# Hybrid trunk kernel: the start of the mixers block, the state copy on ScalarE, the last layer norm, and turnings of the identity between the first tile's products

## The reference, cut to what matters

```python
proj = h @ w_in                                   # c_q, k_a, v_a, k_i, w_i, q_b, z_f, i_b, g_b
c_q = rms_norm(c_q, cq_gain)
q_a = (c_q @ w_uq).reshape(B, L, A_HEADS, A_HEAD_DIM)
# (A) indexer: score = sum_h relu(q_i . k_i) * w_i, top 256 keys per query, softmax with ALiBi over them
# (B) HGRN2, chunkwise:
logf = logaddexp(log(lb), log1p(-lb) + log_sigmoid(z_f));  k_b = (1 - lb) * sigmoid(-z_f)
inter = einsum('bhtd,bhde->bhte', qn * exp(b), S)          # S starts at zero
intra = einsum('bhts,bhse->bhte', scores, vn)
S = exp(b_last) * S + einsum('bhsd,bhse->bhde', kn * exp(b_last - b), vn)
o_b = rms_norm(o_b, onorm_gain) * silu(g_b)
mix = concatenate([o_a, o_b]) @ w_out
h = layer_norm(ALPHA * h + mix, ...);  h = layer_norm(ALPHA * h + swiglu(h), ...)
# layer 1: a causal pooling mixer, then again layer_norm, swiglu, layer_norm; the 16 meta rows are dropped
```

## Time and profile before

| | us |
|---|---|
| median of 3 runs | 2665.35 (2661.79 to 2667.26) |
| the profiled execution's own time | 2666.79 |
| its span, first to last instruction | 2665.0 |
| PE busy, with matmuls | 2548.1 (96%) |
| DVE busy | 1290.3 (48%) |
| ACT busy | 844.5 (32%) |
| POOL busy | 1063.0 (40%) |
| mean granted TensorE clock | 0.967 of 2.4 GHz |

### The profile page before, as it was taken

One profiled execution on the slowest core, in us unless ns is written; L12 is line 12 of the kernel. 1 busy time (PEld: TensorE's weight loads), 2 busy tenths in 40 slices (PEclk: granted clock), 3 DMA queues, 4 the chain that ended last, 5 costly groups with the idle time before them and its releaser, 6 DMA issues.

```text
span 2665.0 us, 36229 instructions
## 1 busy us (share of the span) xinstructions
PE 2548.1 (96%) x14090; PEld 2180.5 (82%) x14090; DVE 1290.3 (48%) x2460; ACT 844.5 (32%) x1387; POOL 1063.0 (40%) x624
## 2 busy tenths in 40 slices
PE   7899999789999989999999999999999999999996
PEld 6789999667788778899888777888787888888885
DVE  6789999588886423333333323332232332232224
ACT  3675221333333223222222322322332322332221
POOL 0432213364544414344434433444433444455442
PEclk9899999699999999999999989999998999999998
DMA  4101220333233234333323223233322233333331
GB/s 133 32 17 43 89 92 19 99 92 116 87 107 96 88 103 119 96 95 95 87 72 95 80 63 95 65 110 95 95 79 79 79 101 103 94 91 103 113 103 46
DMA packets 274613, 230.87 MB, mean 87 GB/s; under 512 B 10640, under 2 KB 255440, under 8 KB 274448
## 3 DMA queue, kind: packets, MB, share of 16 engines
q1 hardware_dynamic: 266256, 220.07, 27.7%
q10 hardware_dynamic: 8192, 8.52, 0.9%
HBM read 215.81 MB, written 12.71 MB: 86 GB/s over the span
## 4 chain that ended last, share of the span: by engine, by line
PE 59%; DMA 1%; POOL 1%; DVE 1%; ACT 1%; issue 0%; POOLq 0%; SPq 0%; ACTq 0%; DVEq 0%
PE banks L1959 36%; PE banks L1975 20%; PE banks L1992 1%; PE banks L1997 1%; PE banks L2009 1%; DMA cq_raw<-in_w_up 0%; PE banks L1668 0%; DMA last_draw<-in_w_down 0%; POOL dL L1877 0%; POOL wL L1866 0%; POOL wL L1870 0%; PE banks L1994 0%; DVE y L1641 0%; DVE y L2165 0%; ACT dH L2059 0%
## 5 line engine op out<-in xcount | busy, mean ns | idle before, releaser
L1870 POOL TENSOR_TENSOR wL<-cq_raw,wH 128x2048 fp32r<-128x2048 f32 x87 | 405.7, 4664 | 565.7 <-ACT wH L2053 565.7
L1959 PE MATMUL banks<-hL,wH 128*128 128x512 f32 (+1 forms) x1760 | 618.9, 352 | 5.6 <-ACT hid L2068 5.3
L1959 PE MATMUL banks<-hH,wL 128*128 128x512 f32 (+1 forms) x1760 | 618.0, 351 | 0.0
L1959 PE MATMUL banks<-hH,wH 128*128 128x512 f32 (+1 forms) x1760 | 616.1, 350 | 0.0
L2145 DVE TENSOR_TENSOR hid<-hid,banks 128x512 f32<-128x512 f32 (+1 forms) x110 | 64.3, 585 | 742.8 <-PE banks L1959 639.2
L1959 PEld LDWEIGHTS banks<-hL,wH 128*128 128x128 f32 x1760 | 331.3, 188 | 54.9 <-ACT hid L2068 6.5
L1959 PEld LDWEIGHTS banks<-hH,wL 128*128 128x128 f32 x1760 | 331.2, 188 | 46.4
L1959 PEld LDWEIGHTS banks<-hH,wH 128*128 128x128 f32 x1760 | 331.8, 189 | 44.9
L1877 POOL TENSOR_TENSOR dL<-last_draw,dH 128x1024 fp32r<-128x1024 f32 x88 | 220.8, 2509 | 350.6 <-ACT dH L2059 350.6
L2165 DVE TENSOR_TENSOR y<-y,banks 128x512 f32<-128x512 f32 (+1 forms) x340 | 233.1, 686 | 219.9 <-PE banks L1975 218.8
L1975 PE MATMUL banks<-dH,hidL 128*128 128x512 f32 (+1 forms) x748 | 303.9, 406 | 2.3 <-issue 2.3
(11 more groups left out here) (249 smaller groups left out, 4248.0 us busy)
## 6 DMA issues: line engine op xcount, KB each, us to landing
cq_raw<-in_w_gate SPq DMA_DIRECT2D x88, 512.0 KB, 4.6
cq_raw<-in_w_up SPq DMA_DIRECT2D x88, 512.0 KB, 6.0
last_draw<-in_w_down SPq DMA_DIRECT2D x88, 512.0 KB, 3.4
w_out_part<-in_w_out SPq DMA_DIRECT2D x60, 512.0 KB, 4.0
va<-in_w_in SPq DMA_DIRECT2D x10, 1024.0 KB, 5.5
va<-in_x SPq DMA_DIRECT2D x8, 512.0 KB, 4.4
vg_scratch<-y ACTq DMA_DIRECT2D x32, 128.0 KB, 1.7
y<-in_x SPq DMA_DIRECT2D x8, 512.0 KB, 7.5
```

What stands on the lines that cost most here:

```text
L1870: nc.gpsimd.tensor_tensor(wL[:, ff % 2, :, :, :].rearrange("p g k f -> p (g k f)"), raw[:, :, :, :].rearrange("p g k f -> p (g k f)"), wH[ ...
L1959: last = nc.tensor.matmul(banks[:, GU + (2 * q + g) % 3, 0:n], wt[:, ff % 2, g, k, :], h[:, k, a:a + n], start=(k == 0 and part == 0), sto ...
```

## The change

It has five parts.

1. `w_uq` is loaded in `projection`, into a part of `y` that is free there (`w_qa0`), and scaled there by ScalarE behind the bank copy of the eighth last unit. In `mixers`, tile 0's `qa` reads it there, and a transfer copies it to `w_qa` for the other tiles. The loads of `y` wait for that copy.
2. The start of `mixers`: the fills of `zt` and `qt` go; `gates` of tile 0 work on the 64 columns that carry data (`own`); VectorE fills half of `key`, `qaT`, and after the gates `S`; GpSimd fills `vt`, `gt`, `qp`.
3. `out` of tile 0 leaves out the product with the old state, which is zero.
4. In every tile ScalarE copies the shared job of step 3 (`state`) ahead of the exponentials.
5. The last norm: ScalarE copies the gain into two PSUM banks in phase 3, VectorE multiplies from there, and for the last tile adds the bias itself, in two halves, each with a store of its own.

And TensorE turns the identity into a bank that nobody reads: once ahead of tile 0's `qa`, 14 times behind it, and 7 times behind each of tile 0's first four steps. `qa` now comes ahead of `gram` level 0.

```diff
@@ projection
+            if j == len(SLABS) - 2:
+                sp.dma_start(w_qa0, ins["w_uq"][0].rearrange("(k p) f -> p k f", p=P)).then_inc(w_qa_loaded, 16)
...
+                if m == len(slab_units) - 8:
+                    act.wait_ge(w_qa_loaded, 16)
+                    for h in range(A_HEADS):
+                        at = w_qa0[:, :, h * HD:(h + 1) * HD]
+                        nc.scalar.activation(at, at, ACT.Copy, scale=HD ** -0.5 / SLOPES[h]).then_inc(w_qa_scaled, 1)
@@ mixers, SyncE
-        sp.dma_start(w_qa[:, :, :], ins["w_uq"][0].rearrange("(k p) f -> p k f", p=P)).then_inc(w_loaded, 16)
-        sp.wait_ge(pads, 1)
         load_z(0)
-        sp.wait_ge(pads, 2)
         load_q(0)
-        sp.wait_ge(pads, 5)
+        sp.dma_start(w_qa[:, :, :], w_qa0).then_inc(w_loaded, 16)
+        sp.wait_ge(pads, 3)
...
+        sp.wait_ge(w_loaded, 16)
+        sp.wait_ge(shared_psum, nth["qa", 0])
         for m in range(5):
             load_y(m)
@@ mixers, GpSimd
-        nc.gpsimd.memset(zt[:, :], PAD_Z).then_inc(pads, 1)
-        nc.gpsimd.memset(qt[:, :], 0.0).then_inc(pads, 1)
-        nc.gpsimd.memset(qp[:], 0.0).then_inc(pads, 1)
         nc.gpsimd.memset(vt[:, 0, :], 0.0).then_inc(pads, 1)
         nc.gpsimd.memset(gt[:, :], 0.0).then_inc(pads, 1)
-        pool.wait_ge(pads, 5)
+        nc.gpsimd.memset(qp[:], 0.0).then_inc(pads, 1)
+        pool.wait_ge(pads, 3)
@@ mixers, TensorE
+                        if m:
+                            nc.tensor.matmul(banks[:, SHARED, h * HD:(h + 1) * HD], qp[:, s, par, f * P:(f + 1) * P],
+                                             state[:, f, par * HD:(par + 1) * HD], start=True, stop=False)
                         last = nc.tensor.matmul(banks[:, SHARED, h * HD:(h + 1) * HD], S[:, s, h, :],
-                                                vt[:, s, h * HD:(h + 1) * HD], start=False, stop=True)
+                                                vt[:, s, h * HD:(h + 1) * HD], start=(m == 0), stop=True)
...
+        def idle(n):
+
+            for _ in range(n):
+                nc.tensor.transpose(banks[:, T_HI, 0:P], ident[:, :], ident[:, :])
+
+        idle(1)
+        on_shared("qa", 0)
+        idle(14)
         gram(0, 0)
-        on_shared("qa", 0)
         for i, (m, h) in enumerate(steps):
             if i < NU:
                 qk(i)
                 if i and h <= levels_of(m):
                     gram(m, h)
+                if m == 0 and h < levels_of(m):
+                    idle(7)
@@ mixers, ScalarE
-        gates(0, 2)
-        gates(0, 3)
-        act.wait_ge(w_loaded, 16)
-        for h in range(4):
-            scaled(h)
-        gates(0, 4)
-        gates(0, 5)
-        for h in range(4, A_HEADS):
-            scaled(h)
+        for stage in (2, 3, 4, 5):
+            gates(0, stage)
         off_shared("qa", 0)
...
-            early = shared_job(m, h) if h == 5 else None
+            early = shared_job(m, h) if h in (3, 5) else None
@@ trunk, the last norm
+            if ph.nth == 3 and i == HALF + 2:
+                act.wait_ge(n3.gb_loaded, 32)
+                for half in range(2):
+                    at = slice(half * 512, (half + 1) * 512)
+                    nc.scalar.activation(gain_bank[:, at], n3.gb[:, at], ACT.Copy).then_inc(gain_kept, 1)
...
+    def gains_from(self, dve, j, gain, halves=False):
+
+        m = self.tiles[j]
+        dve.wait_ge(self.scaled, j - self.before + 1)
+        if not halves:
+            self.nc.vector.tensor_tensor(self.y[:, m, :], self.y[:, m, :], gain, ALU.mult).then_inc(self.gained, 1)
+            return
+        for half in range(2):
+            at = slice(half * 512, (half + 1) * 512)
+            self.nc.vector.tensor_tensor(self.y[:, m, at], self.y[:, m, at], gain[:, at], ALU.mult).then_inc(self.gained_half, 1)
+            dve.wait_ge(self.gained_half, half + 1)
+            self.nc.vector.tensor_tensor(self.y[:, m, at], self.y[:, m, at], self.bb[:, at], ALU.add).then_inc(self.biased_half, 1)
```

More of the change, by code:

```diff
@@ L60 @@
 LEVELS = 7
+SLOPES = [2.0 ** (-8.0 * (h + 1) / A_HEADS) for h in range(A_HEADS)]
 ROUNDS_AHEAD = {NT - 2: 8, NT - 1: 0}
@@ L133, in build, with projection @@
             trunk(nc, c, sem, sb, banks, ident, ins, y, hH, hL, raw, draw, out)
-def projection(nc, c, sem, sb, banks, ident, x, meta, w_in_v, ins, score, cqT, kaT, va, y, qz_dram, vg_dram, kiT, masks):
+def projection(nc, c, sem, sb, banks, ident, x, meta, w_in_v, ins, score, cqT, kaT, va, y, qz_dram, vg_dram, kiT, masks, w_qa0):
     NX = 3
@@ L675, in _, with mixers @@
                 nc.vector.match_replace(at, top8[:, m, :], at, TAKEN).then_inc(late_taken, 1)
-def mixers(nc, c, sem, sb, banks, ident, x, meta, ins, score, masks, cqT, kaT, va, y, qz_dram, vg_dram, raw, draw):
+def mixers(nc, c, sem, sb, banks, ident, x, meta, ins, score, masks, w_qa0, cqT, kaT, va, y, qz_dram, vg_dram, raw, draw):
     W = 4 * P
@@ L707, in mixers @@
     dist = sb(c, "dist", [P, L])
-    SLOPES = [2.0 ** (-8.0 * (h + 1) / A_HEADS) for h in range(A_HEADS)]
     zt = sb(c, "zt", [P, W])
@@ L1092, in on_shared @@
             if what == "qa":
-                if m == 0:
-                    pe.wait_ge(w_scaled, A_HEADS)
+                if m == 1:
+                    pe.wait_ge(w_loaded, 16)
+                w = w_qa if m else w_qa0
                 for ft in range(4):
                     for k in range(QC):
-                        last = nc.tensor.matmul(banks[:, SHARED, ft * P:ft * P + n], w_qa[:, k, ft * P:(ft + 1) * P],
+                        last = nc.tensor.matmul(banks[:, SHARED, ft * P:ft * P + n], w[:, k, ft * P:(ft + 1) * P],
                                                 cqT[:, k, t0:t0 + n], start=(k == 0), stop=(k == QC - 1))
@@ L1752, in trunk @@
                                                    sem("mixed"), sem("tail_kept"))
-    stored = sem("stored")
+    stored, gain_kept = sem("stored"), sem("gain_kept")
+    gain_bank = banks[:, PB:PB + 2, :].rearrange("p b f -> p (b f)")
     HALF = 4
@@ L1855, in _ @@
                 store(i - 4)
-        for j in range(HALF, 2 * HALF):
+        for j in range(HALF, 2 * HALF - 1):
             store(j)
-        sp.wait_ge(stored, 16 * 2 * HALF)
+        t0 = TILES[NT - 1][0] - N_META
+        for half in range(2):
+            at = slice(half * 512, (half + 1) * 512)
+            sp.wait_ge(n3.biased_half, half + 1)
+            sp.dma_start(out[0, t0:t0 + P, at], y[:, NT - 1, at]).then_inc(stored, 16)
+        sp.wait_ge(stored, 16 * (2 * HALF + 1))
     @block.gpsimd
@@ L2235, in _, with last_adds @@
                     n2.low(dve, T - 8)
-        for T in range(HALF + 2):
-            if T < HALF:
-                for half in range(2):
-                    add(NPAIR - 1, 2 * T + half)
-                dve.wait_ge(y_added, PH[-1].down(PAIRS - 1, 2 * T + 1) + 1)
-                n3.stats(dve, HALF + T)
-            if 1 <= T <= HALF:
-                n3.factors(dve, HALF + T - 1)
-            if T >= 2:
-                n3.gains(dve, HALF + T - 2)
+        def last_adds(T):
+            for half in range(2):
+                add(NPAIR - 1, 2 * T + half)
+            dve.wait_ge(y_added, PH[-1].down(PAIRS - 1, 2 * T + 1) + 1)
+            n3.stats(dve, HALF + T)
+        last_adds(0)
+        last_adds(1)
+        n3.factors(dve, HALF)
+        last_adds(2)
+        n3.factors(dve, HALF + 1)
+        dve.wait_ge(gain_kept, 2)
+        n3.gains_from(dve, HALF, gain_bank)
+        last_adds(3)
+        n3.factors(dve, HALF + 2)
+        n3.gains_from(dve, HALF + 1, gain_bank)
+        n3.factors(dve, HALF + 3)
+        n3.gains_from(dve, HALF + 2, gain_bank)
+        n3.gains_from(dve, HALF + 3, gain_bank, halves=True)
 def kernel(**inputs):
```

57 lines of the change are left out of this document (31 added, 26 removed).

## The result

| kernel | median, us | runs | ratio to before | 95% interval |
|---|---|---|---|---|
| before | 2665.99 | 2661.79 to 2667.26 | | |
| changed | 2640.12 | 2637.32 to 2645.20 | 0.9910 | 0.9893 to 0.9927 |

The change takes 25.9 us off. The profiled execution of the changed kernel took 2645.20 us (span 2643.5, clock 0.971), 5.1 above the median: its trace shows less of the gain than the runs do.

What follows compares the result with a forecast made beforehand. Outside full TensorE stretches, three places bound it: the start of `mixers`, step 3's waits for the `state` copy, and the tail. 5.0 + 9.0 + 2.5 = 16.5 us off 2666.79; 2649.5 chosen between 2650.3 and 2648.9; range 2643.5 to 2658.

Steps and rivals of the forecast that it cites:

- Start: Start of `mixers`: earlier `gram` of tile 1 and shorter `out` of tile 0 save 5.0 us at VectorE; bounds 2.3 to 7.5.
- The copy of `state`: Step 3 of each tile: copying ahead of the exponentials removes TensorE's waits, worth 9.0 us; bounds below 3 to 12.1.
- The clock behind these waits: TensorE's low clock after waits for the `state` copy: 1.5 us, counted only in the upper bound of 12.1.
- Tail: Last layer norm after TensorE's last product: gain read from PSUM and halved last tile save 2.5 us; bounds 1.5 to 4.3.
- The sum: Whole kernel: 5.0 + 9.0 + 2.5 = 16.5 us off the profiled 2666.79; forecast 2649.5, chance 0.52.
- The range: Whole kernel: from 2643.5, 1.5 below B, to 2658, halfway between A alone and A with C.
- rival B: Tile 0 and tail: clock rises and stays up into tile 1, 2.5 more; tail not held up, 1.8 more; 2645, chance 0.13.
- A: Step 3: the early `state` copy gives little, as TensorE then waits for VectorE's maxima; 3 us, about 2655.5, chance 0.19.
- C: Start of `mixers`: gives nothing, as q's transfers and GpSimd's chain set the same time; 5.0 less, 2654.5, chance 0.12.
- D: Each tile's step 3: ScalarE's early copy waits for the product, delaying exponentials; slower, about 2669.5, chance 0.04.
- E: Start: turnings don't count for TensorE's clock, so it stays low; start worth 5.0 us; within the forecast's 0.52 chance.

Runs made afterwards that it cites:

- e1: The changed kernel run again with no edit: 2642.10 us, ratio 0.9911 to the kernel before.
- e11: The changed kernel run a third time with no edit: 2639.13 us, ratio 0.9907 to the kernel before.
- e8: The kernel before with only the copy of `state` moved ahead of step 3's exponentials: 2649.94 us, ratio 0.9940.
- e6: The changed kernel with all 32 instructions of tile 0's `out` again, including the product with the zero state: 2642.22 us, ratio 0.9904.
- e2: The changed kernel without the 43 turnings of the identity: 2639.59 us, ratio 0.9905 to the kernel before.
- e4: The changed kernel with the copy of `state` put back behind step 3's exponentials: 2657.25 us, ratio 0.9964.
- e10: The changed kernel with twice the turnings, 28 ahead of tile 0's first `gram` and 14 in each of four steps: 2647.38 us, one run.
- e12: The changed kernel with tile 1's q loaded early and twice the turnings (28, then 14 in each of four steps): 2644.44 us, ratio 0.9923.
- e7: The changed kernel with everything of `trunk` and its norms as before: 2643.26 us, ratio 0.9915.

## Why the prediction was wrong

By its own steps:

- **Start, 5.0 us at VectorE: right.** 5.29 at the scaling of tile 0's values, 5.07 from the sixth maximum of tile 1 on. `gram` at 510.03 (I said 510.5 in one place and 510.7 in another), q at 510.0, the clock low through tile 0 in the first trace, `out` in 3.5 us. In e1 and e11 the clock was up for a few us of tile 0, and it changed nothing: VectorE's second maximum of tile 1 comes 36.2 and 36.0 us behind GpSimd's first instruction in the block, as in the first trace (36.0; before 38.6). The load and the scaling of `w_uq` in `projection`, which I put at nothing, don't show: that first instruction comes at 479.8 to 482.2 in the traces that have them there, and at 480.1 and 480.2 in before and e8. No run takes the parts of the start out one by one, but for `out` (e6) and the turnings (e2); e4, which keeps start and tail and not the copy, is 9.6 us faster than before, where the traces' terms make 8.1. One detail fell: `z`, issued 0.67 earlier, was there no earlier (483.95 against 483.71), so the gates ended at 485.6 and not 484.8; by e2 it was the turnings that kept it, and without them the gates end at 483.6. I took turnings to be free as long as q is late, but they make q late as well: leaving them out wins 2.0 us at VectorE's second maximum of tile 1 (514.01 in e2, 516.00 in the changed kernel).
- **The copy of `state`, 9.0 us: this is the step that failed.** I took each wait at what VectorE lost: 4.3 and 2.85 for the two longest, and 1.9, "less than half", of the four others, since VectorE was nearly full there. Measured in e8, 5.12, 3.40 and 4.0. The whole of TensorE's waits came back, because VectorE ran dry behind them too: for 4.32 and 2.85 us in the two long cases, and for 0.77 and 0.88 in those of tiles 3 and 4, which I had halved. That VectorE is busy for 86% of 650 to 690 didn't mean that it was what tile 4 waited for. With the copy ahead both engines are full at the place of the longest wait, here in e1:

```profile
720.00:730.00 10.00, 9.97 (x68) 8.99 (x68) 9.90 (x21) 4.51 (x13) 5.10 (x8) 1.00 0.40 123
```

- **The clock behind these waits.** I counted 1.5 us for it, once, and only as the upper bound (12.1). In e4 it fell behind both long waits and cost 1.7 and 2.8. That brings the term from 12.5 to 15.5; the medians say 15.2 and 16.1, with an interval of 12 to 20 on the latter.
- **Tail, 2.5 us: right, a little small.** 3.02 in the first pair, 19.3 against 16.3 us in all the others. The multiplication out of PSUM took 1.21 (I said 1.3), the half's addition met GpSimd and took 2.56. One slip in my working: by the earlier trace rows the last tile is scaled at 2653.97, not 2654.05.
- **The sum.** 5.1 + 15.2 to 16.1 + 3.0 is 23 to 24; three comparisons of the changed kernel say 24.8 to 27.9. The parts add up: e4, which has the start and the tail alone, is 9.6 below before, and e8 16.1, together 25.7. What is left over the traces' terms, 1.5 us for start and tail and 2 in the whole, is no more than the medians move from one comparison to the next.
- **The range.** It went to 2643.5 because I let rival B, the clock in tile 0 and the tail, set its low end. B didn't happen: in no trace of the changed kernel did the clock stay up into tile 1, and its tail was held up. The state copy's upper bound, 12.1, gives 5.0 + 12.1 + 2.5 and 2647.2, which lies in the range, and even my three upper bounds together, 7.5 + 12.1 + 4.3, give 2642.9 and not 2640.12. What the range lacked was a copy worth 15 to 16, that is, all waits and the clock falling behind both long ones.

Rivals A and C are out by e8 and by `gram` at 510.03. D, ScalarE held by the product, is out: in tile 5's step its copy waits 0.66 us and the exponentials behind it then wait 2.10 more for VectorE's maximum. E, the page's rule, gave the right number for the start, but not for its reason. Of turnings the Trainium skill, "TensorE: Matmul & The Clock Gate", Part 4, says that "HAM K=8/8 doesn't engage for transpose-mode". The traces say otherwise: e10's and e12's 28 turnings end with the clock at 1.00, and 14 turnings a step, in place of 7, keep it there.

The Trainium skill, "SBUF — State Buffer", section "SBUF: two separate sides", puts VectorE's wait for the shared port on operations with two SBUF inputs beside a GpSimd operation that reads SBUF. The trace agrees: 2.56 us beside GpSimd for what takes 0.69 alone, and 1.21 beside it with the second input in PSUM.

## What to carry to other kernels

Where two engines feed each other and both look 80 to 90% busy, a wait of the one can be paid by the other too: look whether the other engine stands idle behind each wait. Where it does, take the wait whole, not by half; the distance between matching instructions of two traces shows it come back. Behind long waits of TensorE, here 3.45 and 3.17 us, look at how long the products behind them took: the clock fell there in three of four cases, so the median of many runs holds some of that cost though one trace may not show it. And before filling a hole with work that nobody reads, see what real work lies behind the last thing in it: here four pieces of the next tile's projection, with q loaded early, were worth 6 us against the changed kernel, and the turnings cost 2 us in the trace, where a packet of instructions came ahead of the first data.

## What was not expected of the hardware

TensorE's clock falls in `trunk` too, most of it in dense work, at the same ten places or so of the program in nearly every trace, for stretches that differ between executions. Windows of before, of the changed kernel and of e7 over the same 100 us, in which TensorE is busy throughout:

```profile
1460.00:1560.00 100.00, 100.00 (x403) 78.98 (x402) 31.85 (x56) 30.96 (x32) 44.97 (x13) 0.90 0.22 63
```

```profile
1460.00:1560.00 100.00, 100.00 (x415) 79.43 (x414) 26.63 (x44) 31.43 (x32) 42.25 (x14) 0.93 0.27 78
```

```profile
1460.00:1560.00 100.00, 100.00 (x420) 79.02 (x418) 26.61 (x44) 26.67 (x28) 36.52 (x11) 0.94 0.26 74
```

Added up over `trunk`, the time at the low clock is between 64.9 (e7) and 78.5 us (before, e1, e4, e6) in 14 traces, and the length of `trunk` between 1645.7 and 1655.8. Less half of the low time, since work at 0.50 takes twice as long, it is 1612.8 to 1615.0 in all but e10 and e12 (1618.3 and 1619.1): the same work, and up to 7 us of clock. Single runs of one kernel lie 3 to 15 us apart in the table above; the clock in `trunk` would account for up to 7 of that. One pair of traces can't be subtracted to better than this unless the low stretches are counted.
